# Page keys turned on VectorE in 32x32 blocks, and all copies and scaling of new-token probabilities on ScalarE, in a two-layer decoder trunk

## What is computed

```python
def latent_scores(q_lat, q_rope, ckv, kr):
    s = jnp.einsum('nthc,nsc->nhts', q_lat, ckv) + jnp.einsum('nthr,nsr->nhts', q_rope, kr)
    return s.astype(F32) * MLA_SCALE

def mla_sample_attend(q_lat, q_rope, ckv_new, kr_new, ckv_past, kr_past):
    s_past = latent_scores(q_lat, q_rope, ckv_past, kr_past)
    s_new = latent_scores(q_lat, q_rope, ckv_new, kr_new)
    p = jax.nn.softmax(jnp.concatenate([s_past, s_new], axis=-1), axis=-1)
    return (jnp.einsum('nhts,nsc->nthc', p[..., :P], ckv_past)
            + jnp.einsum('nhts,nsc->nthc', p[..., P:], ckv_new))
```

## Time and profile before

| what | value |
|---|---|
| median of three runs | 2794.82 us |
| the profiled execution's span | 2804.0 us, about the slowest of the three runs (2804.56) |
| TensorE busy | 2691.9 us, 96% |
| VectorE busy | 1723.8 us, 61% |
| ScalarE busy | 1111.5 us, 40% |
| POOL busy | 1239.7 us, 44% |
| chain of waits | TensorE 72%, VectorE 14%, issue 4%, ScalarE 3% |
| mean granted TensorE clock | 0.987 |

### The profile page before, as it was taken

How to read it: one execution, slowest core, us unless ns; L and a number is a source line. 1 busy time by engine, 2 the same in 40 slices (tenths; PEclk the granted TensorE clock), 3 DMA queues, 4 the chain that set the end, 5 groups by cost and what they waited for, 6 DMA issues and landing times.

```text
span 2804.0 us, 61530 instructions
## 1 busy us (share of the span) xinstructions
PE 2691.9 (96%) x21801; PEld 2491.0 (89%) x21801; DVE 1723.8 (61%) x3199; ACT 1111.5 (40%) x2499; POOL 1239.7 (44%) x1296
## 2 busy tenths in 40 slices
PE   6999999998999999999899999999998999999998
PEld 5898999998999999999887787878788999999998
DVE  4677678665333336896546666666675434358984
ACT  5121212354444445442543333333364444444444
POOL 3000000455555566544753333333376666665544
PEclk8999999999999999999999999999999999999999
DMA  7422111635666754743133434343453343547442
GB/s 258 144 77 91 48 46 38 208 125 155 204 202 205 213 180 151 260 167 95 54 111 110 148 105 143 105 145 118 147 176 96 118 145 117 150 155 253 165 144 105
DMA packets 385187, 397.91 MB, mean 142 GB/s; under 512 B 27587, under 2 KB 346678, under 8 KB 383046
## 3 DMA queue, kind: packets, MB, share of 16 engines
q1 hardware_dynamic: 362994, 363.57, 41.0%
q10 hardware_dynamic: 13780, 23.05, 2.3%
q0 software_dynamic: 8192, 8.40, 1.0%
HBM read 291.46 MB, written 103.48 MB: 141 GB/s over the span
## 4 chain that ended last, share of the span: by engine, by line
PE 72%; DVE 14%; issue 4%; ACT 3%; POOL 2%; SPq 2%; DMA 2%; DVEq 0%; ACTq 0%; POOLq 0%
PE bank L4068 18%; PE bank L4069 18%; PE bank L4070 17%; PE bank L4691 3%; PE bank L4811 2%; PE bank L4705 2%; DVE xT L3552 1%; DVE stage L3523 1%; DVE td L3529 1%; DVE xT L3545 1%; PE bank L4197 1%; PE bank L4732 1%; POOL op_l L1407 1%; PE bank L4359 1%; PE bank L4797 1%
## 5 line engine op out<-in xcount | busy, mean ns | idle before, releaser
L1407 POOL TENSOR_TENSOR op_l<-raw,op_h 128x512 fp32r<-128x512 f32 (+1 forms) x396 | 518.7, 1314 | 419.8 <-ACT op_h L2076 405.4
L4068 PE MATMUL bank<-t_high,op_h 128*128 128x258 f32 x1736 | 497.7, 287 | 15.2 <-ACT tq L2104 7.5
L4069 PE MATMUL bank<-t_low,op_h 128*128 128x258 f32 x1736 | 493.3, 284 | 0.0
L4070 PE MATMUL bank<-t_high,op_l 128*128 128x258 f32 x1736 | 490.7, 283 | 0.0
L4068 PE MATMUL bank<-hh,whi 128*128 128x344 f32 (+3 forms) x1324 | 436.5, 330 | 20.1 <-POOL hl L1302 4.3
L4070 PE MATMUL bank<-hh,wlo 128*128 128x344 f32 (+3 forms) x1324 | 419.9, 317 | 0.0
L4069 PE MATMUL bank<-hl,whi 128*128 128x344 f32 (+3 forms) x1324 | 419.4, 317 | 0.0
L4068 PEld LDWEIGHTS bank<-t_high,op_h 128*128 128x128 f32 x1736 | 329.2, 190 | 29.1 <-issue 23.4
L4069 PEld LDWEIGHTS bank<-t_low,op_h 128*128 128x128 f32 x1736 | 331.0, 191 | 0.0
L4070 PEld LDWEIGHTS bank<-t_high,op_l 128*128 128x128 f32 x1736 | 330.5, 190 | 0.0
L4068 PE MATMUL bank<-td,op_h 128*128 128x258 f32 x1008 | 289.2, 287 | 18.4 <-DVE xT L3552 15.1
(11 more groups left out here) (521 smaller groups left out, 6241.4 us busy)
## 6 DMA issues: line engine op xcount, KB each, us to landing
raw<-in_w_gu SPq DMA_DIRECT2D x84, 512.0 KB, 4.6
pk<-in_cache_ckv SPq DMA_DIRECT2D x256, 128.0 KB, 2.4
ada_x<-in_w_ada SPq DMA_DIRECT2D x28, 1024.0 KB, 8.4
act_high<-st_all SPq DMA_DIRECT2D x86, 258.0 KB, 5.3
act_low<-st_all SPq DMA_DIRECT2D x86, 258.0 KB, 5.2
act_raw<-tq SPq DMA_DIRECT2D x164, 129.0 KB, 4.0
raw<-in_w_down SPq DMA_DIRECT2D x48, 384.0 KB, 4.3
wst<-in_w_in_even SPq DMA_DIRECT2D x28, 512.0 KB
```

The lines of the kernel that those rows point to most:

```text
L1407: nc.gpsimd.tensor_tensor(op_l[p][:, 0:t.half, :], op_source(p, t), op_h[p][:, 0:t.half, :].bitcast(F), ALU.subtract).then_inc(op_lo.sem, 1)
L4068: mm(out, wh_, xh_, start=start, stop=False, skip_group_check=more)
L4069: mm(out, wh_, xl_, start=False, stop=False, skip_group_check=more)
L4070: return mm(out, wl_, xh_, start=False, stop=stop, skip_group_check=more)
```

## The change

Key turning leaves TensorE. VectorE transposes in blocks of 32x32, straight from the loaded page into `keyb`: token group i (32 tokens) of every page stays on partitions 32i to 32i+31, with 32 channels now on the partitions inside it. Scores then contract 32 channels for four token groups at once, against queries laid out as a block diagonal (`qbd_k`, `qbd_r`: 32 rows and 8 heads for each i, zero elsewhere). That takes 8 latent blocks and 2 rotary blocks, times 4 page groups, 40 matmuls with 32 weight columns and 64 moving columns each. The maximum is over 64 columns instead of 256. The exponential reads the 64 columns four times over, so that after the turning on TensorE a mask (`blk`) leaves each token group's own rows, and page values have 32 output rows instead of 8; sums are divided by 4 at the end.

The block queries are made twice in a stretch by VectorE (`query_blocks`) from a repeated copy, which SP makes with 24 small copies inside SBUF (`queries_repeated`), before the first stretch and, for each later one, in step 4 of the one before. ScalarE takes over the scaling by the reciprocal and the copies of turned probabilities, and has no key copies left. The fills of bank 5 by keys and rotary keys are gone, with their waits.

```diff
+def key_block(j):
+    return (j % CT) * (P // GB) + j // CT
...
+            def queries_repeated(r):
+                if r > 0:
+                    sp.wait_ge(q_ready, 3 * r)
+                for i in range(CG):
+                    rows = slice(i * GB, (i + 1) * GB)
+                    for jj in range(P // GB):
+                        sp.dma_start(qrep[rows, CT * jj:CT * jj + CT], qall[jj * GB:(jj + 1) * GB, 0:CT, 2 * r:2 * r + 2, :]
+                                     ).then_inc(qrep_in.sem, 16)
+                    for jj in range(RB):
+                        sp.dma_start(qrep[rows, KB + jj], qall[jj * GB:(jj + 1) * GB, CT, 2 * r:2 * r + 2, :]).then_inc(qrep_in.sem, 16)
...
                 sp.wait_ge(knew_ready, 1)
+                queries_repeated(0)
                 tokens_saved()
                 page_step(0, 1)
...
                             page_step(r, d + 2)
+                        if r < PAIRS - 1 and d == 4:
+                            queries_repeated(r + 1)
...
+                def normalised(u):
+                    act.wait_ge(*share_ready(u0 + u + 1))
+                    p = pp[u % 2][:, 0:(q + 1) * P]
+                    nc.scalar.mul(p, p, amx[u % 2][:, 3:4]).then_inc(pn_ready, 1)
...
+            def query_blocks(r, n):
+                if n == 0:
+                    dve.wait_ge(*qrep_in(16 * CG * (P // GB + RB) * (r + 1)))
+                on = blk[:].unsqueeze(1).unsqueeze(3)
+                for dst, first, end in ((qbd_r[:], KB, QB), (qbd_k, 0, KB)):
+                    ins = v.tensor_tensor(dst, qrep[:, first:end, n, :].unsqueeze(2).to_broadcast([P, end - first, CG, MH]),
+                                          on.to_broadcast([P, end - first, CG, MH]), ALU.mult)
+                ins.then_inc(q_ready, 1)
...
+            def ropes_out(r, d):
                 dve.wait_ge(ds_ready, r * (CG * STEPS) + CG * d + 1)
+                for half in range(2):
+                    dve.wait_ge(rope_in[2 * (d % 2) + half], 64 * (r * (STEPS // 2) + d // 2 + 1))
+                    v.transpose(keyrt[:, half], pr[2 * (d % 2) + half][:].rearrange("p g c -> p (g c)")).then_inc(key_ready.sem, 1)
+
+            def keys_out(r, d, half):
+                dve.wait_ge(page_in[2 * (d % 2) + half], 16 + 64 * (r * (STEPS // 2) + d // 2 + 1))
+                v.transpose(keyt[half], pk[2 * (d % 2) + half][:].rearrange("p g c -> p (g c)")).then_inc(key_ready.sem, 1)
...
             def page_scores(r, d):
-                filled(r, "keys", d, 3)
+                pe.wait_ge(*key_ready(keys_turned(r * STEPS + d)))
...
-                for part_ in range(CT + 1):
+                for j in range(QB):
                     for g in range(CG):
-                        ins = mm(bank[6][g * GC:g * GC + MH, 0:2 * P], q, k, start=part_ == 0, stop=part_ == CT)
+                        ins = mm(bank[6][g * GC:(g + 1) * GC, 0:NEWS].rearrange("p (a b) -> p a b", a=2),
+                                 (qbd_k[:, j] if j < KB else qbd_r[:, j - KB]).rearrange("p i h -> p (i h)"), k, start=j == 0, stop=j == QB - 1)
```

More of the change, by code:

```diff
@@ L160, in row_tiles, with keys_turned, ropes_turned @@
     return KT
[L163 to L166, removed]
+FILLS = [("probs", _d) for _d in range(STEPS)] + [("peaks",), ("weights",), ("sums",)]
 FILL = {key: i for i, key in enumerate(FILLS)}
 NF = len(FILLS)
+GB = P // CG
+KB = CT * P // GB
+RB = ROPE // GB
+QB = KB + RB
+NEWS = 2 * GB
+def key_block(j):
+    return (j % CT) * (P // GB) + j // CT
+def keys_turned(s):
+    return 4 * s + 4
+def ropes_turned(s):
+    return 4 * s + 2
 def unit(u):
@@ L490, in trunk @@
         last_sq[5] = [rs, sw[0], sw[1]]
+        os_at = used["keep"]
         os32 = lay("keep", "os32", [P, MH, NS])
@@ L513, in trunk @@
         xsd = lay("keep", "xsd", [P, KT, NS])
+        qbd_r = nc.alloc_sbuf_tensor_at("qbd_r", [P, RB, CG, MH], F, offset=at0 + os_at)
+        blk = nc.alloc_sbuf_tensor_at("blk", [P, CG], F, offset=at0 + used["late"])
+        selh = nc.alloc_sbuf_tensor_at("selh", [P, MH], F, offset=at0 + used["late"] + 32)
         used["lat"] = used["pair"] = used["tail"] = used["keep"]
@@ L2541, in probs, with turned @@
                                          scale=MLA_SCALE, accum_out=amx[u % 2][:, 2:3]).then_inc(p_ready, 1)
+                def normalised(u):
+                    e, q, small = unit(u)
+                    act.wait_ge(*share_ready(u0 + u + 1))
+                    p = pp[u % 2][:, 0:(q + 1) * P]
+                    nc.scalar.mul(p, p, amx[u % 2][:, 3:4]).then_inc(pn_ready, 1)
+                def turned(u):
+                    e, q, small = unit(u)
+                    act.wait_ge(pt_bank[0], u0 + u + 1)
+                    act.wait_ge(ao_ready, u0 + u + 1)
+                    w = min(q + 1, 4)
+                    nc.scalar.copy(pt[u % 2][:, 0:w, :], bank[2][:, 0:w * P].rearrange("p (b q) -> p b q", b=w)
+                                   ).then_inc(pt_out[0], 1)
                 def late_turned(u):
@@ L3967, in pairs @@
             def pairs():
+                block_masks()
                 query_low(0, 0, 2)
@@ L4671, in filled @@
                 pe.wait_ge(fill_out, r * NF + FILL[key] + 2)
-            def ropes(r, d):
-                for half in range(2):
-                    pe.wait_ge(rope_in[2 * (d % 2) + half], 64 * (r * (STEPS // 2) + d // 2 + 1))
-                fill(r, "ropes", d)
-                for i in range(4):
-                    two = pr[2 * (d % 2) + i // 2][:, 2 * (i % 2):2 * (i % 2) + 2, :].rearrange("p j c -> p (j c)")
-                    ins = nc.tensor.transpose(bank[5][:, i * P:(i + 1) * P], two, ident[:])
-                ins.then_inc(fill_ready, 1)
@@ L4683, in keys @@
-            def keys(r, d, f):
-                if f % 2 == 0:
-                    pe.wait_ge(page_in[2 * (d % 2) + f // 2], 16 + 64 * (r * (STEPS // 2) + d // 2 + 1))
-                fill(r, "keys", d, f)
-                for e in range(2):
-                    page = pk[2 * (d % 2) + f // 2][:, f % 2 * 2 + e, :]
-                    for ct in range(CT):
-                        ins = nc.tensor.transpose(bank[5][:, (2 * e + ct) * P:(2 * e + ct + 1) * P], page[:, ct * P:(ct + 1) * P], ident[:])
-                ins.then_inc(fill_ready, 1)
@@ L4730, in page_values @@
                     for g in range(CG):
-                        out = bank[6][g * GC:g * GC + MH, 2 * P:4 * P]
-                        mm(out, ptd[:, half * CG + g, :], pk[2 * (d % 2) + half][:, g, :], start=half == 0, stop=half == 1
+                        out = bank[6][g * GC:(g + 1) * GC, 2 * P:4 * P]
+                        mm(out, ptd[:, half, g * GC:(g + 1) * GC], pk[2 * (d % 2) + half][:, g, :], start=half == 0, stop=half == 1
                            ).then_inc(pv_ready, 1)
```

131 lines of the change are left out of this document (61 added, 70 removed).

## The result

The changed kernel takes 2819.8 us (median of 10 runs), the kernel before took 2797.3 in the same session: a ratio of 1.0066, with a 95% interval of 1.0051 to 1.0081. The forecast was 2779 us and "faster". The time lies inside the range, at its upper end, and the direction was wrong.

What follows compares the result with a forecast made beforehand. VectorE's loop through the second key turning would end each attention step, in place of busy TensorE. -34 + 9 + 5 + 4 = -16 us gave 2788 profiled, 2779 us against the median; range 2750 to 2820.

Steps and rivals of the forecast that it cites:

- What leaves and comes to TensorE: In each attention step, 20 transposes (2.1 us) leave TensorE; page scores become 80 matmul passes taking 1.1 us, 2.2 at most.
- turnings: VectorE's new transposes in each step: two of 128x1024 at 1.22 us and two of 128x256 at 0.43 us.
- VectorE's sum: VectorE's busy time in an attention stretch: 30 us in for some 31 out, staying near 61 us.
- A: Rival: a 4-byte turning takes two cycles, each key half costs 2.4 us, so slower at 2846 us; chance 0.16.
- rival B: Hardly a change: page scores take 2.0 to 2.2 us by weight loads, about 1.0 us a step added, 2811 us; chance 0.14.
- The step of 10.3 us: Each of a stretch's eight attention steps shortens from 11.62 us to 10.3, the sum around the loop through VectorE's second key turning.
- the 34 us for four stretches: Gain in the attention stretches from shorter steps: 8.6 us per stretch, 34 us for four.
- What stands in the loop: The list of work from one second key turning to the next, with page scores beside the first terms; sum 10.3 us.
- ScalarE's scaling as two terms of the loop: In each step's loop, ScalarE's scaling by reciprocals counts 0.91 us for the 768-column unit and 0.48 for the small one.
- Term (a): Before the first stretch, the wait for 24 query copies on SP costs 9 us (6 to 13).
- Term (b): In SP's queue, 24 copy issues between the pages of steps 6 and 7 delay last pages in three stretches: +5 us.
- Term (c): TensorE's clock falls to 1.2 GHz around waits and thinned work: +4 us, bounds 0 and 15.

Runs made afterwards that it cites:

- e1: The changed kernel without the 24 query copies for each of pairs 1 to 3, which then use the first pair's queries: 2785.4 us.
- e3: The changed kernel with all query copies made by VectorE and none on SyncE: 2784.5 us, 0.9935 of the kernel before.
- e6: e3 with the second half's key turning made twice in each of the 32 steps: 2842.9 us, 58 us above e3.
- e4: e3 with the first key turning moved to right behind the rope turnings, ahead of the masked copy of page probabilities: 2761.1 us, 23 us below e3.
- e5: e3 with the scaling of new-token probabilities and the copies of their turned first halves back on VectorE: 2789.9 us, ratio 0.9953 to the kernel before.
- e2: The changed kernel with later pairs' query copies spread, six behind each of four steps' page loads instead of 24 behind one: 2813.1 us.
- e8: The changed kernel with the same 24 copy issues a pair, each carrying half its elements: 2822.5 us, ratio 1.0086 to the kernel before.

## Why the prediction was wrong, point by point

- **What leaves and comes to TensorE, turnings, VectorE's sum**: right. The turning measured 1.238 us (1.22), the small one 0.423 (0.43), page scores about 1.2 (1.1); VectorE's busy time fell by 13.2 us in all, some 3 a stretch, where the forecast had 1. Rivals A and B, which hung on these two prices, are out.
- **The step of 10.3 us and the 34 us for four stretches**: right in size. Page scores start at 1538.14 and, three steps on, at 1569.05, so 10.3 us a step; e1 and e3 come to 32 to 37 us under before once the copies are priced. e6 and e4 show the mechanism: a turning taken twice changes a step by its length, and one moved into idle time by most of it.
- **What stands in the loop**: one piece was wrong, and the sum held by luck. The forecast led from the second key turning over the low part of the output (0.29), the reciprocal (0.15) and ScalarE's scaling (0.91) to the transposes, 1.35 us, with the page scores beside them. In the changed kernel's chain of waits it is the other way round:

```profile
1557.63 1.26 DVE keyb L3822
...
1558.93 1.32 PE bank L4750 x80
1560.26 0.81 PE bank L4843 x6
```

The page scores lie on the path with 1.32 us, and the scaling ends beside them, at 1560.09. Both ways take the same here. Slower page scores, as in rival B, would have cost their full excess and not the part that B gave them.
- **ScalarE's scaling as two terms of the loop**: a miss without consequence. The first lies beside the page scores, as just said; with both on VectorE (e5) the loop is as long.
- **Term (a), +9 us**: mis-sized. The step that failed is "an issue lasts 0.30 to 4.45 / 8 = 0.56 us". An issue of these 32-partition copies lasts 0.65 with its gap, 24 of them 15.6; the wait was 16.3 us, not 10.7, so the term is 15, above its upper bound of 13.
- **Term (b), +5 us, "the last pages may come 0 to 3 us late in three stretches"**: this failed, and it alone turned the sign. The issue's price was wrong here too, and the sentence set 7 to 13 us of issues against a whole step of 10.3, as if the queue were empty otherwise. It was not: page issues and the reads of page numbers fill 8.8 us of it, so 17.4 us of copies put the loads 16.2 us back, and the 5.4 us by which the pages had been early (e1) leave 11 us of wait. Measured: 33.7 us by the waits, 34.4 us by e1.
- **Term (c), +4 us for the clock**: right in size. The third step of the second stretch takes 11.70 us at a granted clock of 0.85, where its neighbours at full clock take 10.60 and 10.10, and the same step of the first stretch 10.19. The third and fourth stretches have one such step each, so about 4.5 us lie there, outside the waits. Why the clock falls in just this step is not shown; in e2, with the same work in it, it takes 10.19 in the second and third stretch:

```profile
1685.20:1695.80 10.60, 8.74 (x141) 7.13 (x140) 7.35 (x20) 5.34 (x15) 4.28 (x8) 1.00 0.44 132
1695.80:1707.50 11.70, 10.11 (x140) 8.47 (x140) 7.23 (x20) 5.18 (x14) 4.73 (x9) 0.85 0.36 110
```

- **The sum**, by the starts of page scores in the two traces: the first ones come 14.5 us later (a). From the first to the last of a stretch the four stretches give 34.4 us less, without the page waits; in that the 4.5 us of (c) are already lost, so that the steps at full clock give 39, five more than forecast. The three steps with a page wait take 21.6, 21.7 and 21.3 us where the same step of the fourth stretch takes 9.3, so the waits with what follows them cost 36.7 (b). The rest adds 1. -39 + 4.5 + 14.5 + 36.7 + 1 = +17.7, and the spans differ by +17.8.

The list of rivals missed the one that happened: a slower case by SyncE's queue was not among them, although two terms of the sum stood in that queue.

## What to carry to other kernels

Before work is added to a queue, add up what the queue holds in one turn of the loop: issues, register reads and waits, also those that no row counts as busy. What is left over, with the time by which the loads are early, is the slack, not the length of the turn. The small copies here were paid by the issue, so let an engine that idles at that place make them; and a costly instruction belongs where its engine waits, while one that already falls into idle time gains nothing by a move.

## What the runs showed that was not expected

- A DMA of 32 partitions within SBUF, with 64 or 128 bytes for each, holds SyncE for 0.60 us, 0.65 with the gap, longer than a page load of 128 partitions with 1 KB each (4.02 us for eight). Half the bytes make no difference (e8).
- A VectorE copy of 32 partitions by 16 or 32 columns, most with a shift of partitions, lasts 0.17 us, and the 24 for a pair of samples take 5.0 us; as 24 multiplications in two passes for one sample they take TensorE 0.60 us, 1.2 for both.
- VectorE took 57 us more work (e5) with no change of the time that is clear of noise, though 17% of the changed kernel's chain of waits lies on it.
